# Convolution's fourth tile as ScalarE products added by GpSimd, and three strips' lower parts on GpSimd

## What is computed

```python
z = h @ w_in[i] + b_in[i]
u, v, val, gate = jnp.split(z, [D_A, 2 * D_A, 2 * D_A + D_B], axis=-1)
y_a = spatial_gating_mixer(gelu(u), gelu(v), a_ln_g[i], a_ln_b[i], a_spatial_w[i], a_spatial_b[i])
# conformer_conv_mixer(val, gate, ...):
y = val * sigmoid(gate)
y = causal depthwise convolution of y, width 31, conv_w: (31, 512), + conv_b
y = layernorm(y in 8 groups of 64); y_b = silu(y)
y = concatenate([rmsnorm(y_a), rmsnorm(y_b)]); x = x + gate1 * (y @ w_out[i])
```

## Time and profile before

| | us |
|---|---|
| median of 3 runs | 762.26 (761.32 to 763.24) |
| span of the profiled execution | 769.1 |
| busy: TensorE | 709.7 (92%) |
| busy: weight loads | 561.9 (73%) |
| busy: VectorE | 361.4 (47%) |
| busy: ScalarE | 325.2 (42%) |
| busy: GpSimd | 61.2 (8%) |

### The profile page before, as it was taken

One profiled execution on the slowest core, in us unless ns is written; L12 is line 12 of the kernel. 1 busy time (PEld: TensorE's weight loads), 2 busy tenths in 40 slices (PEclk: granted clock), 3 DMA queues, 4 the chain that ended last, 5 costly groups with the idle time before them and its releaser, 6 DMA issues.

```text
span 769.1 us, 13134 instructions
## 1 busy us (share of the span) xinstructions
PE 709.7 (92%) x5455; PEld 561.9 (73%) x5456; DVE 361.4 (47%) x718; ACT 325.2 (42%) x690; POOL 61.2 (8%) x72
## 2 busy tenths in 40 slices
PE   4889999999999999999999999997999999879786
PEld 2685768887999999999988777876875555344352
DVE  2459967447545555444579589444431111111011
ACT  2365734726444443334566895857321111001011
POOL 0400002000000002000000028162000000000000
PEclk9899999989999999999898999999989999989997
DMA  9998979409667644455453346568869999999996
GB/s 335 354 404 336 370 290 334 157 23 375 218 238 240 222 164 166 169 176 164 164 198 132 124 141 196 164 219 356 308 271 422 421 421 419 420 421 419 421 408 216
DMA packets 75683, 211.44 MB, mean 275 GB/s; under 512 B 7463, under 2 KB 34245, under 8 KB 61798
## 3 DMA queue, kind: packets, MB, share of 16 engines
q1 hardware_dynamic: 74578, 209.91, 72.4%
q0 software_dynamic: 800, 0.63, 0.5%
q10 hardware_dynamic: 244, 0.03, 0.0%
HBM read 209.51 MB, written 1.05 MB: 274 GB/s over the span
## 4 chain that ended last, share of the span: by engine, by line
PE 65%; DMA 13%; DVE 10%; ACT 6%; SPq 3%; issue 2%; ACTq 0%; DVEq 0%
PE ps L1974 10%; PE ps L1975 9%; PE ps L1976 9%; PE ps L2699 6%; PE ps L1987 4%; PE ps L1988 4%; PE ps L1989 4%; DMA ring<-in_expert_w_up_dram 4%; DMA ring<-in_expert_w_gate_dram 4%; DVE YT L1341 3%; DVE ring_low L1225 3%; DMA Z<-in_expert_w_up_dram 3%; SPq L457 3%; PE ps L2668 3%; PE ps L2741 3%; DMA ring<-in_w_in_dram 2%
## 5 line engine op out<-in xcount | busy, mean ns | idle before, releaser
L1225 DVE TENSOR_TENSOR ring_low<-ring,HI 128x1024 fp32r<-128x1024 f32 (+1 forms) x119 | 142.0, 1236 | 27.0 <-ACT HI L712 26.9
L712 ACT ACTIVATE HI<-ring 128x1024 fp32r<-128x1024 f32 (+1 forms) x135 | 133.5, 1055 | 29.0 <-DMA ring<-in_w_in_dram 29.0
L1974 PE MATMUL ps<-AH,HI 128*128 128x256 f32 x320 | 90.1, 282 | 0.3 <-DVE Z L1492 0.3
L1976 PE MATMUL ps<-AH,ring_low 128*128 128x256 f32 x320 | 89.6, 280 | 0.0
L1975 PE MATMUL ps<-AL,HI 128*128 128x256 f32 x320 | 89.5, 280 | 0.0
L2699 PE MATMUL ps<-ring,ZM 128*32 128x256 f32 x880 | 72.7, 421 | 13.7 <-DMA ring<-in_expert_w_up_dram 10.7
L1974 PE MATMUL ps<-HI,AH 128*128 128x512 f32 (+1 forms) x176 | 71.7, 407 | 2.0 <-DVE ring_low L1225 1.0
L1975 PE MATMUL ps<-ring_low,AH 128*128 128x512 f32 (+1 forms) x176 | 69.1, 392 | 0.0
L2699 PEld LDWEIGHTS ps<-ring,ZM 128*32 128x32 f32 x880 | 34.6, 120 | 41.2 <-DMA ring<-in_expert_w_up_dram 14.1
L1987 PE MATMUL ps<-AH,HI 128*128 128x256 f32 x192 | 57.7, 301 | 7.3 <-DVE AL L1311 5.7
L1976 PE MATMUL ps<-HI,AL 128*128 128x512 f32 (+1 forms) x160 | 62.6, 391 | 0.0
(11 more groups left out here) (394 smaller groups left out, 1293.6 us busy)
## 6 DMA issues: line engine op xcount, KB each, us to landing
ring<-in_expert_w_up_dram SPq DMA_DIRECT2D x28, 1024.0 KB, 24.7
ring<-in_expert_w_gate_dram SPq DMA_DIRECT2D x27, 1024.0 KB, 26.2
ring<-in_expert_w_down_dram SPq DMA_DIRECT2D x24, 1024.0 KB, 23.9
ring<-in_w_ffn_in_dram SPq DMA_DIRECT2D x20, 1024.0 KB, 6.5
ring<-in_w_in_dram SPq DMA_DIRECT2D x18, 1024.0 KB, 6.0
ring<-in_ada_w_dram SPq DMA_DIRECT2D x16, 1024.0 KB, 9.1
ring<-in_w_ffn_out_dram SPq DMA_DIRECT2D x11, 1024.0 KB, 7.1
ring<-in_ada_w_dram SPq DMA_DIRECT2D x16, 512.0 KB, 11.1
```

What stands on the lines that cost most here:

```text
L712: act(HI[:, (i + 1) % UNITS, 0:w], W.view(name)[:, o:o + w], ACT.Copy).then_inc(s_hi, 1)
L1225: tt(W.low(name)[:, o:o + w], W.view(name)[:, o:o + w], HI[:, (i + 1) % UNITS, 0:w].bitcast(F32), ALU.subtract).then_inc(s_lo, 1)
L1974: mm(dst, lh, rh, start=start, stop=False)
L1976: return mm(dst, ll, rh, start=False, stop=stop)
```

## The change

`CV[:, 3]` is no more a sum on TensorE. ScalarE makes the 31 products of a shifted view of YC with a tap's weights, the first with the bias directly into `CV[:, 3]`, the others into four places `TP`; GpSimd adds them one by one, each waiting for its product and for the add before, and ScalarE waits for a place to come free. `DM`, the diagonals on TensorE and the semaphores `s_dm`, `s_dp` go. The lower parts of `in_u0` to `kv_v1`, twelve units, move from VectorE's list to GpSimd's, between its adds; GpSimd's table loads stand behind them. `lo_to` on VectorE passes over them by `pooled`, as it does with the names already there.

```diff
@@ -114,7 +114,9 @@
         return self.all[u][0] in POOLED
 
 
-POOLED = ("pool0", "pool1", "attn0", "attn1", "wq0", "wq1", "wo0", "wo1")
+POOLED1 = ("in_u0", "in_u1", "in_w0", "in_w1", "kv_v0", "kv_v1")
+POOLED2 = ("pool0", "pool1", "attn0", "attn1", "wq0", "wq1", "wo0", "wo1")
+POOLED = POOLED1 + POOLED2
 
 
 def split_order():
@@ -267,7 +269,7 @@
         V = Zf[:, 1024:2048].rearrange("p (t n) -> p t n", t=2)
         SQY, GQ = tiles(Zf[:, 0:1024], 4), tiles(Zf[:, 1024:2048], 4)
         CV, SG = YT[:, 0:4, :], YT[:, 4:8, :]
-        DM = tiles(flat2(YT[:, 4:8, :]), 8)
+        TP = YT[:, 4:8, :]
         YC = flat2(SR1[:, :, :])[:, 0:4 * 286].rearrange("p (c n) -> p c n", c=4)
         RTS, RGS = [st[:, 28 + 2 * i:30 + 2 * i] for i in range(5)], st[:, 40:56]
         blk = flat2(QT[:, :, :])[:, 0:P]
@@ -361,7 +363,7 @@
 
         s_rp, s_rc = sem("s_rp"), sem("s_rc")
 
-        s_glu, s_sg, s_yc, s_tap, s_dm, s_dp, s_cv3 = (sem(n) for n in ("s_glu", "s_sg", "s_yc", "s_tap", "s_dm", "s_dp", "s_cv3"))
+        s_glu, s_sg, s_yc, s_tap, s_tp, s_cv3 = (sem(n) for n in ("s_glu", "s_sg", "s_yc", "s_tap", "s_tp", "s_cv3"))
         s_wtp, s_wt, s_e = (sem(n) for n in ("s_wtp", "s_wt", "s_e"))
         s_uv, s_tn, s_mn, s_mtp, s_mh, s_ml = (sem(n) for n in ("s_uv", "s_tn", "s_mn", "s_mtp", "s_mh", "s_ml"))
         s_mxp, s_mx, s_my, s_vm, s_ks = (sem(n) for n in ("s_mxp", "s_mx", "s_my", "s_vm", "s_ks"))
@@ -654,6 +656,32 @@
             po.memset(blk[0:64, :][:, 0:64], 1.0 / 64).then_inc(s_set, 1)
             po.memset(blk[64:128, :][:, 64:128], 1.0 / 64).then_inc(s_set, 1)
 
+            def lower(u0, u1):
+                for u in range(u0, u1):
+                    if S.pooled(u):
+                        name, o, w = S.all[u]
+                        po.wait_ge(s_hi, u + 1)
+                        po.tensor_tensor(W.low(name)[:, o:o + w], W.view(name)[:, o:o + w], HI[:, (u + 1) % UNITS, 0:w].bitcast(F32),
+                                         ALU.subtract).then_inc(s_lp, 1)
+
+            def taps_added(i):
+
+                for j in range(max(5 * i, 1), min(5 * i + 5, TAPS)):
+                    po.wait_ge(s_tp, j)
+                    po.wait_ge(s_cv3, j)
+                    po.tensor_tensor(CV[:, 3, :], CV[:, 3, :], TP[:, (j - 1) % 4, :], ALU.add).then_inc(s_cv3, 1)
+
+            po.wait_ge(s_set, BLK)
+            iu = S.first["in_u0"]
+            lower(iu, iu + AHEAD + 1)
+            taps_added(0)
+            lower(iu + AHEAD + 1, iu + AHEAD + 3)
+            for i in range(1, 6):
+                taps_added(i)
+                lower(iu + AHEAD + 2 + i, iu + AHEAD + 3 + i)
+            taps_added(6)
+            lower(iu + AHEAD + 8, S.end["kv_v1"])
+
             po.wait_ge(s_mxp, 2)
             const(rope[:, 0, :, :], A["cos"].rearrange("(t p) d -> p t d", p=P), s_c3)
             const(rope[:, 1, :, :], A["sin"].rearrange("(t p) d -> p t d", p=P), s_c3)
@@ -671,12 +699,7 @@
                                      bc(hn[:, i, hi:hi + 32], 1, [P, NT, 32]), ALU.mult).then_inc(s_tab, 1)
 
             po.wait_ge(s_hk, 8)
-            for u in range(len(S.all)):
-                if S.pooled(u):
-                    name, o, w = S.all[u]
-                    po.wait_ge(s_hi, u + 1)
-                    po.tensor_tensor(W.low(name)[:, o:o + w], W.view(name)[:, o:o + w], HI[:, (u + 1) % UNITS, 0:w].bitcast(F32),
-                                     ALU.subtract).then_inc(s_lp, 1)
+            lower(S.first[POOLED2[0]], len(S.all))
 
             po.wait_ge(s_wr, 32)
             po.wait_ge(s_r2, 16 * LOADS2)
@@ -796,17 +819,21 @@
 
             iu, iw = S.first["in_u0"], S.first["in_w0"]
 
-            def diagonals(i):
+            def products(i):
 
                 for j in range(5 * i, min(5 * i + 5, TAPS)):
-                    if j >= 8:
-                        ac.wait_ge(s_dp, j - 7)
-                    act(DM[:, j % 8, :], ident[:, :], ACT.Copy, scale=cw[:, 3, j:j + 1]).then_inc(s_dm, 1)
+                    src = YC[:, 3, j:j + 256]
+                    if j == 0:
+                        act(CV[:, 3, :], src, ACT.Identity, scale=cw[:, 3, 0:1], bias=C1[:, CB + 3:CB + 4]).then_inc(s_cv3, 1)
+                        continue
+                    if j > 4:
+                        ac.wait_ge(s_cv3, j - 3)
+                    act(TP[:, (j - 1) % 4, :], src, ACT.Copy, scale=cw[:, 3, j:j + 1]).then_inc(s_tp, 1)
 
             hi_to(iu + AHEAD)
             ac.wait_ge(s_rc, 3)
             ac.wait_ge(s_yc, 4)
-            diagonals(0)
+            products(0)
             hi_to(iu + 1 + AHEAD)
             ac.wait_ge(s_mem, 32)
             for t in range(NT):
@@ -819,27 +846,27 @@
                     act(JM, MX[t][:, 512 * n:512 * n + 512], ACT.Square, scale=1.0 / 32,
                         accum_out=mst[:, 2 * t + n:2 * t + n + 1]).then_inc(s_mn, 1)
             hi_to(iu + 2 + AHEAD)
-            diagonals(1)
+            products(1)
             hi_to(iu + 3 + AHEAD)
-            diagonals(2)
+            products(2)
             ac.wait_ge(s_t0, T0["u1"])
             act(V[:, 0, :], ps[4][:, :], ACT.Gelu).then_inc(s_uv, 1)
             ac.wait_ge(s_un, S.end["in_u1"])
             act(V[:, 1, :], ps[5][:, :], ACT.Gelu).then_inc(s_uv, 1)
             hi_to(iw + AHEAD)
-            diagonals(3)
+            products(3)
 
             ac.wait_ge(s_tn, 4)
             act(st[:, 24:26], st[:, 21:24:2], ACT.Sqrt, bias=eps[:, 0:1]).then_inc(s_tn, 1)
             ac.wait_ge(s_mn, 5)
             act(mst[:, 4:6], mst[:, 4:6], ACT.Sqrt, bias=eps[:, 0:1]).then_inc(s_mn, 1)
             hi_to(iw + 1 + AHEAD)
-            diagonals(4)
+            products(4)
             ac.wait_ge(s_mn, 7)
             for t in range(NT):
                 act(MX[t], MX[t], ACT.Copy, scale=mst[:, 4 + t:5 + t]).then_inc(s_mn, 1)
             hi_to(iw + 2 + AHEAD)
-            diagonals(5)
+            products(5)
             for kk in range(4):
                 ac.wait_ge(s_mtp, kk + 1)
                 for k in (2 * kk, 2 * kk + 1):
@@ -847,14 +874,12 @@
                               scale=C1[:, NM + k:NM + k + 1])
                 ins.then_inc(s_mh, 1)
             hi_to(iw + 3 + AHEAD)
-            diagonals(6)
+            products(6)
             ac.wait_ge(s_un, S.end["in_w1"])
             for ct in range(4):
                 act(U[:, ct, :], ps[ct // 2][:, 256 * (ct % 2):256 * (ct % 2) + 256], ACT.Gelu,
                     bias=C1[:, BU + ct:BU + ct + 1]).then_inc(s_uv, 1)
             warm(ACT.Sqrt)
-            ac.wait_ge(s_dp, TAPS)
-            act(CV[:, 3, :], ps[3][:, 0:256], ACT.Identity, bias=C1[:, CB + 3:CB + 4]).then_inc(s_cv3, 1)
 
             ik, io = S.first["kv_v0"], S.first["out0"]
             hi_to(ik + AHEAD)
@@ -2177,20 +2202,11 @@
             ins.then_inc(s_wtp, 1)
 
 
-            def diagonals(i):
-
-                for j in range(5 * i, min(5 * i + 5, TAPS)):
-                    te.wait_ge(s_dm, j + 1)
-                    mm(ps[3][:, 0:256], DM[:, j % 8, :], YC[:, 3, j:j + 256],
-                       start=(j == 0), stop=(j == TAPS - 1)).then_inc(s_dp, 1)
-
             def between_v(i):
                 if i == 0:
                     te.wait_ge(s_col, 2)
                 for k in ((0, 1), (2, 3), (4, 5), (6, 7))[i]:
                     ada(1, k)
-                if i:
-                    diagonals(i - 1)
 
             te.wait_ge(W.sems[BROW], 16)
             strip(("in_u0", "in_u1"), (4, 5), OP_X, 0, brow_v, between_v, per=2)
@@ -2202,7 +2218,6 @@
                     te.wait_ge(s_col, 3)
                 for k in ((), (0, 1), (2, 3, 4), (5, 6, 7))[i]:
                     ada(2, k)
-                diagonals(3 + i)
                 if i == 2:
                     te.wait_ge(s_mn, 9)
                     te.wait_ge(s_uv, 2)
@@ -2238,7 +2253,7 @@
                 if i == 2:
                     te.wait_ge(s_set, BLK)
                     te.wait_ge(s_tap, 3 * TAPS)
-                    te.wait_ge(s_cv3, 1)
+                    te.wait_ge(s_cv3, TAPS)
                     mm(ps[3][:, :], blk, CV[:, 0:2, :], start=True, stop=True).then_inc(s_gmp, 1)
                     spread(7, 256, 1, SUM_A)
 
```

## The result

The changed kernel took 789.21 us, the median of four runs (787.19 to 790.05); the kernel before took 762.35 beside it (761.32 to 763.24). The ratio is 1.0313, with a 95% interval of 1.0265 to 1.036. The forecast was 785.0, with a range of 767 to 799. Where the runs of one kernel spread, its median here is over all of them, while a ratio and its interval take only those within 1.5% of its fastest. The profiled execution after has a span of 785.4 us against 769.1.

The account below looks back on a forecast made before the run. It took close bounds on TensorE and VectorE, with VectorE's taps taking turns with GpSimd after the change: 769.1 + 22.5 = 791.6 us profiled; the same shift on the 762.26 median gave 784.8, said as 785, range 767 to 799.

Parts of the forecast that it names:

- The cause: VectorE's taps with two SBUF inputs take turns with GpSimd's instructions, so those within the chain lengthen it; chance 0.65.
- no turns for the taps: Rival: taps pass freely beside GpSimd, L2081 stays near 91 and 16 diagonals come off, -7.5, giving 754.8 us; chance 0.10.
- turns only against the long instructions: Rival: adds slip between taps and only lower parts cost, first stage +6.4, total near 769 us; chance 0.10.
- GpSimd keeps the port: Rival: GpSimd holds the port while it has work, waiting taps lose more often, about 5 us more, 790; chance 0.13.
- The first stage: Up to the second columns' transposes (L2081): 90.5 - 6.8 + 27.5 - 1.1 = 110.1 us.
- The second stage: From L2081 to L2242, the product needing the whole convolution: VectorE's chain ends it at 151.4 us, +22.5 against 128.9.
- DMA at 0.92 and 0.85 gets slack, not less: Claim for both stretches: SyncE's loads wait on TensorE's counts and move with it, so DMA gains slack; priced at nothing.
- Rival 1: The rival of freely passing taps; its price was 7.5 us off the second stage for 16 diagonals; chance 0.10.
- The signs in the profile: Taps alternating 0.4 and above 1.0 us, adds above 1.0, TensorE idle some 25 us before L2081, product near 151.
- The sign against it: The forecast is wrong if a tap's mean stays at 0.48, or if L2242's shift shrinks again by the end.
- the first paragraph: Opening step: a shift made before 134 us moves the later expert-weight loads with it to the end, one for one.
- The sum for the profiled execution: The profiled span of 769.1 plus the shift of 22.5 us at L2242, 791.6 us.

Follow-up runs that it names:

- psum_taps: The changed kernel with the running sums of channel tiles 0 and 1 in PSUM, so 60 of 90 taps have one SBUF input; 778.58 us, ratio 1.0078.
- taps_only: The changed kernel with the lower parts of in_u0 to kv_v1 back on VectorE, products and adds as changed; 775.69 us, ratio 1.0149.
- low_only: The kernel before with only the twelve lower parts of in_u0 to kv_v1 moved to GpSimd, diagonals kept on TensorE; 780.45 us, ratio 1.0177.
- the second execution: The changed kernel, unchanged, profiled and timed again: span 789.0 us; timed median 789.58 us, ratio 1.0253 to the kernel before.
- no_adds: The changed kernel with GpSimd's thirty adds left out, ScalarE's products and GpSimd's lower parts kept; 775.81 us, ratio 1.0144.
- psum_order: The changed kernel with tiles 0 and 1 summed in PSUM, second columns early, out0 load behind adaLN loads, YA before the last taps; 763.26 us, ratio 0.997.

## Why the prediction was right, by its own steps

**The cause.** "If they take turns with GpSimd, GpSimd's 12 lower parts and 30 adds aren't beside the chain; those within it are on it": shown by psum_taps. The rival *no turns for the taps* falls with it, and so does *turns only against the long instructions*, since taps_only pays 9.2 us for adds alone. *GpSimd keeps the port* falls too: in the changed kernel one tap comes in behind each GpSimd instruction, and in low_only and taps_only a GpSimd instruction even waited 6.7 and 6.8 us. The extension of the rule in the Trainium skill (SBUF — State Buffer, Who interferes with whom) to scalar_tensor_tensor was right, and so was its other side: with one input from PSUM there was no wait, 484 ns at most.

**The first stage.** Columns were forecast at 110.1 and came at 108.5; from 33.9 us between YC and columns the stage grew by 16.4 where the sum had 19.6. The records, each less its plain length, give all three terms. The nineteen adds cost VectorE 8.5 us, some 0.49 on a tap and less on an instruction from PSUM, where the sum had 13.3 - 1.1 = 12.2: it put an add and a tap end to end, 1.10 us, and their period is 0.89. The six lower parts cost 12.7, 2.1 each, where the sum had 14.2. In the other direction the normalization of v at L1403, which reads a single SBUF tile and writes one, waited behind a GpSimd lower part that began at 105.10: 2.57 us where its twin took 0.55, 2.0 us that the sum had at nothing. 8.5 + 12.7 + 2.0 - 6.8 is 16.4. The same section of the Trainium skill does list tensor_scalar, in its modes that use both pairs of ports; the trace agrees with that. The forecast had passed over it, although its own rows had a tensor_scalar of 4.21 us beside two of GpSimd's lower parts (L1660). GpSimd's nineteenth add was done at 92.4, forecast 96.

**The second stage.** Forecast 41.3 us from columns to product, measured 37.3 (145.8 with the product's weight load) and 39.9 in the second execution. VectorE was quicker by the cheaper adds, and the end was set by something else: the line "DMA at 0.92 and 0.85 gets slack, not less" is the step that failed. The loads wait for counts of a TensorE that stands, so its 23 us become a hole in DMA (0.22 from 91 to 109 us) and a chain of five loads afterwards. The forecast had the wait's cause and length (25 us), said that SyncE's loads move with TensorE's counts, and took that for slack. The clock was priced at 1 to 3 us. After the wait TensorE's first 21 steps of a unit stand 0.21 us apart (109.65 to 113.91) and the last ones 0.12, so that unit lost 2 us, which fits; the 0.50 from 91 to 109 us lies in idle time. The second execution, 2.6 us longer here, has a granted clock of 0.89 from 109 to 149 us where the first has 0.93 from 109 to 147.

**Rival 1's price**, 7.5 us off for sixteen diagonals, was never met. taps_only and no_adds got back 2.3 to 2.7 against the kernel before and 5.1 to 5.5 against low_only; the adaLN loads need their 15.5 to 16.5 us with the diagonals or without them, and TensorE's lower clock behind its wait takes some too. No run takes the diagonals off and leaves the turns out, as that rival supposed; psum_order, with the loads reordered, comes nearest with 5 us.

**The signs in the profile.** Taps of 0.4 beside taps above 1.0: the long ones are 2.6 beside a lower part, but 0.96 beside an add. GpSimd's adds above 1.0: no, 0.74 in the median, 0.91 at most. TensorE idle for 25 us, put down to the copy: 23.0. The product near 151: 146.0. The sign against it, a mean tap of 0.48, did not come: 0.80.

**The rest, and how two errors met.** From the product to the end it is 640.4 us before and 639.6 after: the shift stays to the end, as the first paragraph argued. The sum for the profiled execution was 791.6, and the span 785.4: 6 too long. To come to the median it took off 6.8, since before's profiled execution lay that much above its runs. After's did not: 785.4 against a median of 789.21. That 785 lay so near 789 is thus luck in part: two errors of opposite sign. The shift of the medians (26.9 us) is larger than that of the profiles (16.3). The granted clock (the third figure from the end of a row) shows where the profiles of one kernel differ. Before:

```profile
380.00:400.00 20.00, 19.89 (x79) 15.57 (x79) 14.80 (x30) 11.28 (x25) 0.00 (x0) 0.88 0.48 159
400.00:420.00 20.00, 20.00 (x112) 17.96 (x111) 17.63 (x43) 13.99 (x33) 0.00 (x0) 0.83 0.43 147
```

and the same kernel again:

```profile
380.00:400.00 20.00, 19.78 (x95) 15.71 (x96) 14.98 (x31) 12.57 (x32) 0.00 (x0) 1.00 0.49 159
400.00:420.00 20.00, 20.00 (x115) 17.49 (x114) 18.73 (x45) 15.44 (x37) 0.00 (x0) 0.91 0.48 159
```

The first took 640.4 us from product to end, the second 632.0. The timed runs of before beside all the experiments lie between 760.51 and 773.77 us, with mean clocks between 0.975 and 0.952. All ten of the changed kernel's runs (787.19 to 790.05 and 786.2 to 790.95) have 0.938 to 0.951, and both of its profiles took some 640 us from product to end. About 17 of the 26.9 us are thus the shift at the product and the other 9 or 10 the longer kind of rest. Why the changed kernel was never in the shorter kind stays open: no run here separates it from the shift.

## What to carry to other kernels

Before work is moved to GpSimd, count the VectorE instructions of that stretch which have two inputs in SBUF, and look at the tensor_scalar ones from SBUF to SBUF: against those GpSimd isn't a second engine. Here a GpSimd instruction cost VectorE 0.49 us for an add of 0.74 and 2.1 us for a lower part of 2.4. If the moved work is worth it, first put one operand of VectorE's chain into PSUM. And wherever a change lets TensorE stand, ask which loads wait for its slots, and price the first loads after it restarts.

## What the runs showed of the hardware that was not expected

- Taking turns was unequal: GpSimd's adds kept 740 ns in the median and its lower parts 2400, while a VectorE tap went from 475 ns to 0.96 us beside an add and to 2.6 us beside a lower part. One tap passed for each GpSimd instruction there; but in low_only a single lower part took 9.07 us, and in taps_only a single add 7.54 us, while taps ran on behind each other at 0.40 us.
- A chained add and the tap between them take 0.89 us, less than their records together (0.74 and 0.475).
- A VectorE tensor_scalar with one SBUF tile as input and its output in SBUF waited for GpSimd as well: 2573 ns for 547.
- Two executions of the kernel before differed by 8.4 us behind the product, and the longer one had the lower clock granted in two stretches behind 380 us (0.88 and 0.83 against 1.00 and 0.91). A single profile can lie in either kind, so its distance to the median doesn't carry over to another kernel.
